# Down-projections of two middle blocks as seven block products each, in one sequence with gate and up

## The reference, cut to what matters

```python
def swiglu(x, g, w_gate, w_up, w_down):
    n = rms_norm(x, g)
    return (jax.nn.silu(n @ w_gate) * (n @ w_up)) @ w_down
```

## Time and profile before

| | |
|---|---|
| median of 3 runs | 1440.64 us (1440.4 to 1441.3) |
| profiled execution, first to last instruction (span) | 1438.2 us |
| profiled execution, own device time | not reported apart; the median lies 2.4 us above the span |
| TensorE busy | 1417.6 us, 99% |
| VectorE busy | 955.4 us, 66% |
| ScalarE busy | 662.5 us, 46% |
| granted TensorE clock, mean | 0.999 |

### The profile page before, as it was taken

How to read it: one execution, slowest core, us unless ns; L and a number is a source line. 1 busy time by engine, 2 the same in 40 slices (tenths; PEclk the granted TensorE clock), 3 DMA queues, 4 the chain that set the end, 5 groups by cost and what they waited for, 6 DMA issues and landing times.

```text
span 1438.2 us, 23835 instructions
## 1 busy us (share of the span) xinstructions
PE 1417.6 (99%) x9484; PEld 1341.1 (93%) x9484; DVE 955.4 (66%) x1559; ACT 662.5 (46%) x1302; POOL 156.9 (11%) x110
## 2 busy tenths in 40 slices
PE   7999999999999999999999999999999999999998
PEld 6897878999999999999988878699999999999998
DVE  5658667878785576477445776677787746845853
ACT  5458564334353254254435675633434523523544
POOL 3416010200000000000232241002000000000002
PEclk9999999999999999999999999999999999999999
DMA  5340231233123223121233211213221322231212
GB/s 170 109 117 13 70 85 42 68 97 103 52 89 106 71 85 96 56 89 52 74 86 116 72 55 47 76 45 118 67 88 60 119 76 71 88 95 53 88 45 96
DMA packets 161182, 115.23 MB, mean 80 GB/s; under 512 B 18192, under 2 KB 155792, under 8 KB 161040
## 3 DMA queue, kind: packets, MB, share of 16 engines
q1 hardware_dynamic: 161072, 113.71, 26.5%
HBM read 108.90 MB, written 6.62 MB: 80 GB/s over the span
## 4 chain that ended last, share of the span: by engine, by line
PE 90%; DVE 4%; ACT 3%; DMA 1%; issue 1%; SPq 1%; ACTq 0%
PE ps L602 35%; PE ps L1280 10%; PE ps L1279 10%; PE ps L1278 10%; PE ps L729 3%; PE ps L731 3%; PE ps L730 3%; PE ps L1163 1%; PE ps L1054 1%; ACT pw L1439 1%; PE ps L655 1%; DMA wraw<-w_uq 1%; PE ps L844 1%; PE ps L1080 1%; PE ps L621 1%
## 5 line engine op out<-in xcount | busy, mean ns | idle before, releaser
L1930 DVE TENSOR_TENSOR wlo<-wraw,whi 128x1024 fp32r<-128x1024 f32 (+2 forms) x119 | 128.2, 1078 | 192.2 <-ACT whi L1393 191.9
L1393 ACT ACTIVATE whi<-wraw 128x1024 fp32r<-128x1024 f32 (+2 forms) x119 | 107.6, 911 | 205.8 <-PE ps L602 146.4
L1280 PE MATMUL ps<-tth,ringl 128*128 128x320 f32 x576 | 178.0, 309 | 0.0
L1279 PE MATMUL ps<-tl,ringh 128*128 128x320 f32 x576 | 177.3, 308 | 0.0
L1278 PE MATMUL ps<-tth,ringh 128*128 128x320 f32 x576 | 176.4, 306 | 0.0
L602 PE MATMUL ps<-hh,whi 128*128 128x320 f32 x692 | 157.9, 309 | 0.6 <-DVE xT L2519 0.6
L602 PE MATMUL ps<-hl,whi 128*128 128x320 f32 x692 | 157.7, 309 | 0.0
L602 PE MATMUL ps<-hh,wlo 128*128 128x320 f32 x692 | 157.6, 309 | 0.0
L2399 DVE TENSOR_TENSOR ringl<-sums,ringh 128x512 fp32r<-128x512 f32 x144 | 99.4, 691 | 54.3 <-ACT ringh L1808 52.1
L1279 PE MATMUL ps<-tbl,ringh 128*128 128x320 f32 x432 | 133.5, 309 | 0.0
L1280 PE MATMUL ps<-tbh,ringl 128*128 128x320 f32 x432 | 133.5, 309 | 0.0
(11 more groups left out here) (411 smaller groups left out, 3288.9 us busy)
## 6 DMA issues: line engine op xcount, KB each, us to landing
raw_gate<-w_gate SPq DMA_DIRECT2D x18, 1024.0 KB, 5.4
raw_up<-w_up SPq DMA_DIRECT2D x18, 1024.0 KB, 5.4
wraw<-w_down SPq DMA_DIRECT2D x48, 384.0 KB, 3.4
wraw<-w_out SPq DMA_DIRECT2D x32, 128.0 KB, 2.8
wraw<-w_out SPq DMA_DIRECT2D x16, 256.0 KB, 3.2
wraw<-w_gate SPq DMA_DIRECT2D x8, 512.0 KB, 3.8
wraw<-w_up SPq DMA_DIRECT2D x8, 512.0 KB, 3.8
wraw<-w_down SPq DMA_DIRECT2D x16, 256.0 KB, 3.0
```

The costliest lines, as they stand in the source:

```text
L1279: mm(o, wh[:, c, :], xl[:, c, :], start=False, stop=False, skip_group_check=True)
L1280: ins = mm(o, wl[:, c, :], xh[:, c, :], start=False, stop=c == KH - 1, skip_group_check=True)
L1393: run(whi[:, unit_cols(u)], wraw[:, unit_cols(u)], ACT.Copy).then_inc(unit_hi.sem, 1)
L1930: vec.tensor_tensor(wlo[:, w], wraw[:, w], whi[:, w], ALU.subtract).then_inc(unit_lo.sem, 1)
```

## The change

Blocks 1 and 2 get their down-projection by the same scheme: output chunks are taken in pairs (4 groups for a block, numbered `NG` = 18 to 25), the hidden tiles of a pair of tiles and the two output chunks form the 2 x 2 split on the left, and the two tiles by two token halves form it on the right. Each product has 3 chunks (`DP`) times 3 matmuls of 128 x 320. The steps of gate and up of all blocks and of these down groups are one sequence, `RUN`, with one ring, one look-ahead of 4 and one chain of raw loads. Block 0 and block 3 keep `down_rows`.

The right operands of down are new: for each pair of hidden tiles seven blocks of 320 columns, three of them plain (of `tu`), four of them sums (`t12`, `t34`), each split in a high part (`dhi`) and a low part (`dlo_first`, `dlo_rest`). They take the place of `hh`, `hl` in blocks 1 and 2. The results of down products are added to `xT` one by one, 320 wide, seven for a group (`down_emptied`). `pair` counts pairs of tiles, `in_rows` marks block 3, `final` the last group of gate and up of a block. The two slots of `sums2` replace the four of `sums4`. The diff, cut to its core:

```diff
+def down_products(blk):
+
+    first = NG + KH * (blk - 1)
+    for n in range(first, first + KH):
+        yield n, 1
+        yield n, 5
+        if n > first:
+            yield n - 1, 4
+        yield n, 6
+        yield n, 2
+        yield n, 3
+        yield n, 7
+
+
+RUN = [key for part in (products(1), down_products(1), products(2), down_products(2), products(3)) for key in part]
+LEFTS = [n for n, x in RUN if x == 1]
+PLACE = {n: q for q, n in enumerate(LEFTS)}
...
+                if down and x in (6, 3, 7, 4):
+                    pe.wait_ge(d_new.sem, d_new.at(l, D_NEW[n, {6: 1, 3: 5, 7: 6, 4: 7}[x]]))
+                elif x in (6, 3, 7):
+                    pe.wait_ge(kept.sem, kept.at(l, KEPT[n, {6: 1, 3: 5, 7: 6}[x]]))
+                elif x == 4:
                     pe.wait_ge(c_new.sem, c_new.at(l, C_NEW[n, 7]))
                 if n == 0:
                     pe.wait_ge(right_lo.sem, right_lo.at(l, 2 * KH))
                 pe.wait_ge(a_lo.sem, a_lo.at(l, STEP[n, x] + 1))
...
+                pairs = 4 * DP * ((n - NG) // KH)
+                if down and (n - NG) % KH == 0:
+                    pe.wait_ge(d_lo.sem, d_lo.at(l, pairs + 4 * (DP - 1)))
+                for c in range(DP if down else KH):
+                    if down and c == DP - 1 and (n - NG) % KH == 0:
+                        pe.wait_ge(d_lo.sem, d_lo.at(l, pairs + 4 * (DP - 1) + RIGHT_COUNT[x]))
                     mm(o, wh[:, c, :], xh[:, c, :], start=fresh and c == 0, stop=False, skip_group_check=True)
...
+            for blk in ROWS_IN_PLACE:
+                if blk:
+                    for n, x in RUN:
+                        product(n, x)
...
+            def down_right_hi(q, first, end, source, ready, value):
+
+                act.wait_ge(ready.sem, ready.at(l, value))
+                run(dhi[:, first:end, q % DP, :], source, ACT.Copy).then_inc(d_hi.sem, 1)
...
+                elif up and not in_rows and x in (2, 7, 4):
+                    if x == 2:
+                        down_right_hi(pair, 0, 1, tu[:, 0:1, half(0)], h_new, PLAIN + pair + 1)
+                    if x == (2 if final else 7):
+                        down_right_hi(pair, 1, 3, t12[:, :, :], right_new, 2 * KH + 2 * pair + 1)
+                    if x == 4:
+                        down_right_hi(pair, 3, 5, tu[:, 1, :].rearrange("p (j n) -> p j n", j=2), up_c21, pair + 1)
+                        down_right_hi(pair, 5, 7, t34[:, :, :], right_new, 2 * KH + 2 * pair + 2)
...
+            def down_right_lo(q, first, end, source):
+
+                dve.wait_ge(d_hi.sem, d_hi.at(l, 4 * q + {1: 1, 3: 2, 5: 3, 7: 4}[end]))
+                vec.tensor_tensor(down_low(first, end)[:, :, q % DP, :], source, dhi[:, first:end, q % DP, :], ALU.subtract).then_inc(d_lo.sem, 1)
...
+            def down_emptied(n, x):
+
+                b, g = divmod(n - NG, KH)
+                bx, by, bz = group_banks(n)
+                d, j = {1: (0, 0), 2: (0, 0), 6: (0, 1), 3: (0, 1), 5: (1, 1), 7: (1, 1), 4: (1, 0)}[x]
+                if g == 0 and x == 1:
+                    q = DP * b + DP - 1
+                    down_right_lo(q, 3, 5, hidden_halves(1))
+                dve.wait_ge(a_used.sem, a_used.at(l, STEP[n, x] + 1))
+                if x in (2, 3, 7):
+                    dve.wait_ge(d_new.sem, d_new.at(l, D_NEW[n, {2: 1, 3: 6, 7: 5}[x]]))
+                target = xT[:, 2 * g + d, half(j)]
+                bank = bz if x == 2 else by if x in (5, 3) else bx
+                vec.tensor_tensor(target, ps[:, bank, 0:HALF], target, ALU.add).then_inc(d_new.sem, 1)
+                if g == 0 and x == 1:
+                    down_right_lo(q, 5, 7, t34[:, :, :])
...
+                    if up and not in_rows:
+                        dve.wait_ge(c_new.sem, c_new.at(l, C_NEW[n, 3]))
+                        dve.wait_ge(silu_new.sem, silu_new.at(l, PLAIN + SILU[2 * pair, 2]))
+                        chain("b12", vec.tensor_tensor(tu[:, 0, half(1)], tu[:, 0, half(1)], tg[:, 0, half(1)], ALU.mult))
...
+                    elif up:
+                        vec.tensor_tensor(tu[:, 0, half(0)], tu[:, 0, half(0)], tg[:, 0, half(0)], ALU.mult).then_inc(h_new.sem, 1)
+                        chain_end("b12")
+                        dve.wait_ge(h_new.sem, h_new.at(l, PLAIN + pair + 1))
+                        if pair:
+                            dve.wait_ge(d_lo.sem, d_lo.at(l, 4 * pair))
+                        t1 = vec.tensor_tensor(t12[:, 0, :], tu[:, 0, half(1)], tu[:, 0, half(0)], ALU.subtract)
+                        chain("t1", t1)
+                        if final:
+                            chain_end("t1")
+                            vec.tensor_tensor(t12[:, 1, :], tu[:, 1, half(1)], t12[:, 0, :], ALU.subtract).then_inc(right_new.sem, 1)
...
+                    if up and not in_rows:
+                        chain("b22", b22)
+                        if not final:
+                            down_right_lo(pair, 0, 1, tu[:, 0:1, half(0)])
+                        chain_end("b22")
+                        chain_end("b12")
+                        if pair:
+                            dve.wait_ge(d_lo.sem, d_lo.at(l, 4 * pair))
+                        if not final:
+                            chain_end("t1")
+                            vec.tensor_tensor(t12[:, 1, :], tu[:, 1, half(1)], t12[:, 0, :], ALU.subtract).then_inc(right_new.sem, 1)
+                        vec.tensor_tensor(t34[:, 0, :], tu[:, 1, half(1)], tu[:, 0, half(1)], ALU.subtract)
...
-                    hidden_lo(f, tu[:, 0, :])
+                    if in_rows:
+                        hidden_lo(f, tu[:, 0, :])
+                    elif final:
+                        down_right_lo(pair, 0, 1, tu[:, 0:1, half(0)])
+                    else:
+                        down_right_lo(pair, 1, 3, t12[:, :, :])
                     dve.wait_ge(a_used.sem, done)
                     dve.wait_ge(silu_new.sem, silu_new.at(l, PLAIN + SILU[2 * pair, 4]))
                     vec.tensor_tensor(tu[:, 1, half(0)], ps[:, bx, 0:HALF], tg[:, 1, half(0)], ALU.mult).then_inc(up_c21.sem, 1)
-                elif x == 6 and not up and n > run_start:
+                    if not in_rows:
+                        if final:
+                            down_right_lo(pair, 1, 3, t12[:, :, :])
+                        dve.wait_ge(right_new.sem, right_new.at(l, 2 * KH + 2 * pair + 1))
+                        dve.wait_ge(up_c21.sem, up_c21.at(l, pair + 1))
+                        vec.tensor_tensor(t34[:, 1, :], tu[:, 1, half(0)], t12[:, 1, :], ALU.subtract).then_inc(right_new.sem, 1)
+                elif x == 6 and not up and pair > 2 * DP:
                     hidden_lo(f - 1, tu[:, 1, :])
+                elif x == 6 and not up and pair % DP:
+                    down_right_lo(pair - 1, 3, 5, hidden_halves(1))
+                    down_right_lo(pair - 1, 5, 7, t34[:, :, :])
 
             for i in range(PLAIN):
                 odd, u, base = i % 2, U_FFN + 2 * i, 4 * (i % 2)
```

More of the change, by code:

```diff
@@ L100, in products, with counts @@
             yield n, 4
-def counts(xs, every):
-    keys = [key for blk in range(NBLK) for key in products(blk) if key[1] in xs and key[0] % every == 0]
+def down_products(blk):
[12 more added lines that the diff above has]
+PLACE = {n: q for q, n in enumerate(LEFTS)}
+def counts(xs, every, first=0, end=NG):
+    keys = [key for key in RUN if key[1] in xs and key[0] % every == 0 and first <= key[0] < end]
     return {key: k + 1 for k, key in enumerate(keys)}
-STEP = {key: q for q, key in enumerate(key for blk in range(NBLK) for key in products(blk))}
+STEP = {key: q for q, key in enumerate(RUN)}
 KEPT = counts((1, 5, 6), 1)
@@ L562, in _ @@
                 if i == 1:
-                    load_pair(0)
-            for blk in range(NBLK):
-                first, end = GROUPS_OF[blk]
-                ahead = 2 if blk else 6
-                for d in range(ahead):
-                    load_down(blk, d)
-                if blk == 0:
-                    load_pair(1)
-                for n in range(first, end):
-                    if n + 2 < NG:
-                        load_pair(n + 2)
-                for d in range(ahead, NC_):
-                    load_down(blk, d)
+                    load_left(0)
+            for d in range(6):
+                load_down(0, d)
+            load_left(1)
+            for d in range(6, NC_):
+                load_down(0, d)
+            for q in range(2, len(LEFTS)):
+                load_left(q)
+            sp.wait_ge(a_used.sem, a_used.at(l, STEP[NG + NDOWN - 1, 4] + 1))
+            for d in range(NC_):
+                load_down(3, d)
         for t in range(NT):
@@ L1274, in product @@
                 wh, wl = ring_of(n, x)
-                xh, xl = right_of(x)
-                fresh = x in (1, 5, 2)
-                for c in range(KH):
+                if down:
+                    r = RIGHT_OF[x]
+                    xh, xl = dhi[:, r], down_low(r, r + 1)[:, 0]
```

(6 more changed lines are left out.)

233 lines of the change are left out of this document (137 added, 96 removed).

## The result

The changed kernel takes 1459.1 us (1457.2 to 1459.5, 4 runs) against 1440.6: a ratio of 1.0125, 95% interval 1.0111 to 1.0140. It is slower, on the side that was forecast and inside the range, 7 us above the 1452 of the forecast.

A forecast was written before the change was run, and what follows sets the result against it. TensorE, busy 1417.6 of 1438.2 us, was taken as the bound. Saving 21.8 and adding stalls of 12 and 21 gave 1449.4 of span, plus 2.4 for the median: 1452 us, 0.8% slower, range 1445 to 1460 (8 in 10: 1442 to 1463).

The forecast's parts named there:

- What TensorE saves: Down stages of blocks 1 and 2 become 252 matmuls, 36.80 us for 42.24; 21.8 us less over two layers.
- Stall A: Inside a gate and up pair, TensorE waits before product 4 for product 7's bank: 1.5 us, eight times, 12 us.
- the ScalarE term: In stall A, ScalarE copies two more blocks of 640 (1.3 us); 1.0 counted, plus 0.1 for semaphore steps.
- Stall B: Where gate and up end and down begins, TensorE waits for `dlo_first` of the last pair: 2.55 us, four times.
- Stall C: Two products later, down product 6 waits for product 1's addition to `xT`: 2.7 us, four times.
- The sum: Whole kernel: 1438.2 - 21.8 + 12 + 21 = 1449.4 us of span, median 2.4 above, so 1451.8.
- rival 3: TensorE's clock falls in the block-end stalls, costing 3.5 us at each of 4 ends, 14 more: 1466; chance 0.04.
- Rival 1: Block-end chains are shorter because ScalarE's ring part is not held behind `t12`: faster, 1434 us; chance 0.10.
- rival 2: VectorE bounds throughout, each instruction costing its full duration in pairs and down groups: 12 us more, 1464; chance 0.10.

The follow-up runs named there:

- the last kernel but one: Against the kernel with all three orders, VectorE also adds the first down product to the stream before the last sum of `t34`: 1429.9 us, ratio 0.9923.
- With the clock held: Changed kernel plus 17 extra matmuls, results unused, before each of the two waits at a block end: 1452.2 us, ratio 1.0080.
- the bank first: Against the changed kernel, first down product added to the stream before two low parts, `t34` copied after the next ring part: 1447.8 us, ratio 1.0057.
- both block-end orders: Changed kernel with the edits of the first block early and the bank first together: 1442.1 us, ratio 1.0011.
- all three orders: Changed kernel with the first block early, the bank first and the wide low parts later together: 1433.5 us, ratio 0.9957.
- the wide low parts later: Against the changed kernel, two 640 wide low parts on VectorE moved behind the emptying of product 7 of a gate group: 1448.7 us, ratio 1.0056.
- the first block early: Against the changed kernel, last pair's first right block gets its low part earlier, `t12` copied after the next ring part: 1452.7 us, ratio 1.0083.

## Why the prediction was right, and where it fell short

- **What TensorE saves**, 21.8 us: right. The matmul count is 9340, and with the waits taken away the gain appears (the last kernel but one has ratio 0.9923, which is 11.1 us, and it still has 7.3 us idle in 12 waits, 9.2 from start to start: 20.3).
- **Stall A**, 1.5 us eight times: came eight times in the places named. At 414.44 TensorE starts the product that it would have started at 413.12 (412.84 plus the 0.28 by which the run began later here, at 374.54): 1.3 us. The stretch started 0.5 us earlier, for which I had taken 0.6. It was 3.2 us longer than before; of the ScalarE term, taken as 1.0 plus 0.1, 0.8 is what the rows leave (15.3 - 12.1 - 2.46).
- **Stall B**, 2.55 us: from the matmul before to 454.60 are 2.73 us more than the pace. The mechanism, ring part behind `t12` and `dlo_first` behind the ring part, is the chain in the rows, and putting `dlo_first` first took it away.
- **Stall C**, 2.7 us: 2.4 idle and 0.16 at the one block end that had its full clock when the wait began. At the others it is 0.9, 1.7 and 1.5 idle, since TensorE's slow matmuls came later to the wait.
- **The sum** of the waits was 12 + 21 = 33 us; 28 are there as waits, and at full clock stall C would add 3 more. The lengths of the stages close the sum. With the clock held, the 504 matmuls of a run of gate and up take 76.4 us for 73.6 before, and the 252 of a down stage 42.5 for the 36.8 of the prediction: 2.8 and 5.7 us more at each of four places, 34 in all. A was 0.9 us less in all than I said, B and C together 1.8 more. That the total is so near is in part these two errors against each other.
- **The clock**, rival 3, was the part I thought unlikely (0.04): it fell at all four block ends. Its price was put at 14 us; 6.5 us is what keeping TensorE busy gave back. Two steps failed here. One is the chance: I read "its longest wait now is 2.16 us, and the window around it shows 1.00" as speaking for waits of 2.6 and 2.7 as well, and left the clock out of the sum. That 1.00 didn't even speak for the 2.16 us, since the matmuls around it ran at half their pace (last section). The other is the price: I charged the slow matmuls between B and C in full, but stall C stood behind them and shrank by 3.2 us in all. TensorE: Matmul & The Clock Gate of the Trainium skill (HAM oscillation) said that waits between bursts lower the clock, and these runs agree with it: 0.50 was granted at all four block ends, where TensorE had waited 2.6 us. With the clock held the kernel takes 1452.2, close to my 1452; 6.5 of the 7 us above the forecast are the clock.
- **Rival 1** (shorter chains, faster) and **rival 2** (VectorE the bound throughout, 1464) both fell. The median came nearer to rival 2's time than to mine, but the waits rule it out: in the later down groups TensorE never waits, and moving work without taking any away brought the time from 1459 to 1433. At the block ends alone VectorE's load may be the limit once the order is mended: the wait came back at product 3, behind two wide low parts. Only that one further order was tried, so this is not shown.

## What to carry to other kernels

Fewer matmuls pay only if what feeds them keeps its place: a helper that is busy 89% of the time (VectorE for 21.3 of 24.0 us, 416 to 440 in the changed kernel) can still stop the bound engine when new work stands in front of the one result that it needs next. For each result with one or two steps of slack, list what stands before it on both helper engines, and put copies for later steps behind it. Where a wait of some 2.7 us on TensorE can't be avoided, price its lower clock too, or fill it with matmuls.

## What was not expected of the hardware

The clock fell after waits as short as these, and not each time. In the kernel with the bank first it was at half both in the start of the program, behind a wait of 2.2 us that stands there in every kernel, and at two block ends, the second and the third (windows as above; the third is 1162.3 to 1165.7, also 0.50):

```profile
12.10:15.40 3.30, 3.30 (x9) 2.58 (x8) 2.61 (x4) 2.44 (x4) 1.50 (x1) 0.50 1.04 379
571.90:575.20 3.30, 3.30 (x13) 2.99 (x13) 3.30 (x7) 2.20 (x5) 0.00 (x0) 0.50 0.00 0
```

At its first and fourth block ends the wait for `dlo_first` was as long, 2.6 us, and the clock stayed at 1.00. The windows of five more kernels show a low clock in the same start (all but the changed one, the one with both block-end orders and the changed one kept busy).

In the kernel before, the row of the clock shows 1.00 for this start. The matmuls don't bear it out:

```profile
12.10:15.40 3.30, 2.66 (x6) 2.15 (x7) 2.97 (x4) 3.30 (x6) 0.23 (x1) 1.00 0.91 340
...
12.74 2.47 PE L691 MATMUL ps<-whi,nh 128*128 128x512 f32 x5 [2.16 <-ACT whi L1409]
15.01 1.64 PE L694 MATMUL ps<-whi,nl 128*128 128x512 f32 x5
16.49 1.30 PE L700 MATMUL ps<-wlo,nh 128*128 128x512 f32 x5
17.63 1.47 PE L629 MATMUL ps<-kc,xin 128*128 128x128 f32 x12
```

Five matmuls of 512 columns take 2.27 us from 12.74 to 15.01, 0.45 each, and five take 1.14 us from 16.49 to 17.63, 0.23 each. So behind this wait TensorE ran at half its later pace, and a 1.00 in the row of the clock isn't evidence for these first 16 us. In front of the wait it was slow too: twelve matmuls like those at 17.63, for which 1.47 us are shown, have 2.82 us at 7.76. So the earlier trace rows say nothing of what a wait of 2.2 us does to the clock.

With all three orders, where the waits of a block end are 0.6, 0.5 and 1.0 us idle (0.8, 0.6 and 1.2 from start to start), it still fell at two of four. Counted over the kept profiles it fell at four of four block ends in the changed kernel and in the one with the wide low parts later, at three with the first block early, at two with the bank first, at one with both block-end orders, and at none where TensorE was kept busy. What decides it from one block end to the next stays open.
